# Column sums of squares: adding finished tiles on GpSimd before TensorE sums them

## What is computed

```
x = x + gx1 * _rms_norm(_token_mixer(h, ...), g_post_mix)     # the mixer ends in merged @ w_out
hm = _modulate(x, g_pre_mlp, sx2, cx2)                        # _rms_norm(x) * (1 + scale) + shift
x = x + gx2 * _rms_norm(square(relu(hm @ w1)) @ w2, g_post_mlp)
```

## Time and profile before

| | us |
|---|---|
| timed runs, median of 3 | 4251.79 |
| lowest and highest | 4250.93, 4254.33 |
| the profiled execution | 4245.13 |
| its span, first to last instruction | 4243.4 |
| mean granted TensorE clock in it | 0.917 |

### The profile page before, as it was taken

How to read it: one execution, slowest core, us unless ns; L and a number is a source line. 1 busy time by engine, 2 the same in 40 slices (tenths; PEclk the granted TensorE clock), 3 DMA queues, 4 the chain that set the end, 5 groups by cost and what they waited for, 6 DMA issues and landing times. The chain is left out here.

```text
span 4243.4 us, 47248 instructions
## 1 busy us (share of the span) xinstructions
PE 3803.9 (90%) x18108; PEld 2862.6 (67%) x18108; DVE 1992.6 (47%) x3170; ACT 1441.9 (34%) x2504; POOL 148.6 (4%) x104
## 2 busy tenths in 40 slices
PE   6888898989999999989799998999898877998777
PEld 3888897646777788757556777788786435784435
DVE  1755664655443544316655443544323354333363
ACT  2554333234433222233244433222223433223421
POOL 0000000010000100000100001000100010000010
PEclk9999998999999899899899998999898678997788
DMA  7434452211123222262111122222221000220001
GB/s 292 139 117 152 135 167 101 85 35 45 55 70 100 70 94 95 102 261 99 60 45 45 65 70 85 85 96 98 68 95 60 15 5 30 80 94 25 15 5 60
DMA packets 95535, 362.40 MB, mean 85 GB/s; under 512 B 10976, under 2 KB 11232, under 8 KB 93792
## 3 DMA queue, kind: packets, MB, share of 16 engines
q1 hardware_dynamic: 95328, 359.52, 25.0%
HBM read 352.13 MB, written 7.34 MB: 85 GB/s over the span
## 5 line engine op out<-in xcount | busy, mean ns | idle before, releaser
L365 DVE TENSOR_TENSOR w_lo<-w_raw,w_hi 128x1024 fp32r<-128x1024 f32 x525 | 642.4, 1224 | 932.0 <-ACT w_hi L355 931.6
L379 PE MATMUL banks<-h_hi,w_hi 128*128 128x512 f32 (+1 forms) x2040 | 766.7, 376 | 26.7 <-DVE h_lo L997 9.8
L380 PE MATMUL banks<-h_lo,w_hi 128*128 128x512 f32 (+1 forms) x2040 | 748.0, 367 | 0.0
L381 PE MATMUL banks<-h_hi,w_lo 128*128 128x512 f32 (+1 forms) x2040 | 748.0, 367 | 0.0
L355 ACT ACTIVATE w_hi<-w_raw 128x1024 fp32r<-128x1024 f32 x543 | 570.7, 1054 | 412.1 <-DMA w_raw<-in_stream 404.3
L379 PEld LDWEIGHTS banks<-h_hi,w_hi 128*128 128x128 f32 x2040 | 390.6, 191 | 109.6 <-issue 22.1
L381 PEld LDWEIGHTS banks<-h_hi,w_lo 128*128 128x128 f32 x2040 | 389.3, 191 | 64.8
L380 PEld LDWEIGHTS banks<-h_lo,w_hi 128*128 128x128 f32 x2040 | 390.1, 191 | 60.5 <-issue 0.5
L379 PE MATMUL banks<-merged_hi,w_hi 128*128 128x512 f32 (+1 forms) x960 | 349.9, 364 | 28.5 <-PEq L2312 10.7
L381 PE MATMUL banks<-merged_hi,w_lo 128*128 128x512 f32 (+1 forms) x960 | 346.9, 361 | 0.0
L380 PE MATMUL banks<-merged_lo,w_hi 128*128 128x512 f32 (+1 forms) x960 | 345.7, 360 | 0.0
(11 more groups left out here) (309 smaller groups left out, 5324.9 us busy)
## 6 DMA issues: line engine op xcount, KB each, us to landing
w_raw<-in_stream SPq DMA_DIRECT2D x591, 512.0 KB, 3.5
w_whole<-in_stream SPq DMA_DIRECT2D x48, 512.0 KB, 9.0
x_kept<-x SPq DMA_DIRECT2D x2, 2048.0 KB, 7.5
dft_table<-in_dft SPq DMA_DIRECT2D x2, 2048.0 KB, 8.3
x<-x_kept SPq DMA_DIRECT2D x2, 2048.0 KB, 8.4
x<-in_x SPq DMA_DIRECT2D x1, 2048.0 KB, 12.2
out_x<-x SPq DMA_DIRECT2D x1, 2048.0 KB, 6.2
late_consts<-in_consts SPq DMA_DIRECT2D x1, 1280.0 KB, 5.6
```

The lines of the kernel that those rows point to most:

```text
L365: (by or self.nc.vector).tensor_tensor(self.lo[:, c], self.raw[:, c], self.hi[:, c].bitcast(F32), ALU.subtract)\
L379: self.nc.tensor.matmul(out, w_hi, x_hi, start=start, stop=False)
L380: self.nc.tensor.matmul(out, w_hi, x_lo, start=False, stop=False)
L381: mm = self.nc.tensor.matmul(out, w_lo, x_hi, start=False, stop=stop)
```

## The change

`post_mix` and `post_mlp` get a common tile `squares_total`. GpSimd adds the squares of tiles 0 to 6 into it as they are finished: the first add takes tiles 0 and 1, five more take one tile each (`RowNorm.gather`). TensorE no longer sums each tile. It sums the total behind the last tile of the projection (`sum_gathered`) and then the last tile's squares (`sum_last`), so a norm has two groups of columns in PSUM instead of eight. ScalarE, ahead of square k from the fifth on, waits for GpSimd's add that read the slot. `pre_mlp`, `pre_mix` and `following` stay as they were. On GpSimd's list the gathering for post_mix comes first, the two low parts of chunks move from ahead of the first residual to behind it, and the gathering for post_mlp stands between them and the second residual.

```diff
--- before.py
+++ after.py
@@ -873,18 +873,22 @@
 
 
 
-    def __init__(self, K, name, n_tiles, NT, at, rows_bank):
-        self.K, self.n, self.NT, self.nt = K, n_tiles, NT, NT // P
-        self.sums = K.ps[:, 7, at:at + n_tiles * self.nt]
+    def __init__(self, K, name, n_tiles, NT, at, rows_bank, total=None):
+        self.K, self.n, self.NT, self.nt, self.total = K, n_tiles, NT, NT // P, total
+        self.n_sums = n_tiles if total is None else 2
+        self.sums = K.ps[:, 7, at:at + self.n_sums * self.nt]
         self.rows = K.ps[:, rows_bank, 0:NT]
         self.sq = None
         self.mean, self.rt, self.rstd = (K.take(f"{name}_{t}", [self.nt]) for t in ("mean", "root", "rstd"))
         S = lambda t: K.count_of(f"{name}_{t}")
         self.squared, self.summed, self.averaged = S("squared"), S("summed"), S("averaged")
         self.rooted, self.inverse, self.turned = S("rooted"), S("inverse"), S("turned")
+        self.gathered = S("gathered") if total is not None else None
 
     def square(self, act, k, src):
-        if k >= 4:
+        if k >= 4 and self.total is not None:
+            act.wait_ge(self.gathered.sem, self.gathered.at(max(1, k - 4)))
+        elif k >= 4:
             act.wait_ge(self.summed.sem, self.summed.at(k - 3))
         return self.K.nc.scalar.activation(self.sq[:, k % 4], src, ACT.Square).then_inc(self.squared.sem, 1)
 
@@ -896,8 +900,30 @@
                                          self.K.const("ones")[:, 0:1], start=True, stop=True)
         mm.then_inc(self.summed.sem, 1)
 
+    def gather(self, pool):
+        for k in range(1, self.n - 1):
+            pool.wait_ge(self.squared.sem, self.squared.at(k + 1))
+            if k > 1:
+                pool.wait_ge(self.gathered.sem, self.gathered.at(k - 1))
+            self.K.nc.gpsimd.tensor_tensor(self.total[:], self.sq[:, 0] if k == 1 else self.total[:], self.sq[:, k % 4], ALU.add)\
+                .then_inc(self.gathered.sem, 1)
+
+    def sum_gathered(self, pe):
+        pe.wait_ge(self.gathered.sem, self.gathered.at(self.n - 2))
+        for i in range(self.nt):
+            mm = self.K.nc.tensor.matmul(self.sums[:, i:i + 1], self.total[:, i * P:(i + 1) * P], self.K.const("ones")[:, 0:1],
+                                         start=True, stop=True)
+        mm.then_inc(self.summed.sem, 1)
+
+    def sum_last(self, pe):
+        pe.wait_ge(self.squared.sem, self.squared.at(self.n))
+        for i in range(self.nt):
+            mm = self.K.nc.tensor.matmul(self.sums[:, self.nt + i:self.nt + i + 1], self.sq[:, (self.n - 1) % 4, i * P:(i + 1) * P],
+                                         self.K.const("ones")[:, 0:1], start=True, stop=True)
+        mm.then_inc(self.summed.sem, 1)
+
     def average(self, dve):
-        dve.wait_ge(self.summed.sem, self.summed.at(self.n))
+        dve.wait_ge(self.summed.sem, self.summed.at(self.n_sums))
         self.K.nc.vector.reduce_sum(self.mean[:], self.sums.rearrange("p (k i) -> p i k", i=self.nt), AX_X)\
             .then_inc(self.averaged.sem, 1)
 
@@ -921,9 +947,11 @@
         eng.wait_ge(self.turned.sem, self.turned.at(1))
 
     def close(self):
-        for s, n in ((self.squared, self.n), (self.summed, self.n), (self.averaged, 1), (self.rooted, 1),
+        for s, n in ((self.squared, self.n), (self.summed, self.n_sums), (self.averaged, 1), (self.rooted, 1),
                      (self.inverse, 1), (self.turned, 1)):
             s.advance(n)
+        if self.total is not None:
+            self.gathered.advance(self.n - 2)
         for t in (self.mean, self.rt, self.rstd):
             self.K.give(t)
 
@@ -1024,9 +1052,10 @@
         m = K.sb(scope, "mid", [2, NT])
         sq = K.sb(scope, "squares", [4, NT])
         table = K.sb(scope, "table_load", [1])
-        post_mix = RowNorm(K, "post_mix", KD, NT, 0, 4)
+        total = K.sb(scope, "squares_total", [NT])
+        post_mix = RowNorm(K, "post_mix", KD, NT, 0, 4, total)
         pre_mlp = RowNorm(K, "pre_mlp", KD, NT, 32, 5)
-        post_mlp = RowNorm(K, "post_mlp", KD, NT, 64, 4)
+        post_mlp = RowNorm(K, "post_mlp", KD, NT, 64, 4, total)
         for norm in (post_mix, pre_mlp, post_mlp, following):
             if norm is not None:
                 norm.sq = sq
@@ -1046,9 +1075,8 @@
                 for k in range(KD):
                     W.multiply(pe, K.ps[:, f % 4, 0:NT], (c0 + f) * CHUNK + k, h_hi[:, k, 0:NT], h_lo[:, k, 0:NT],
                                k == 0, k == KD - 1)
-                if f >= 1:
-                    post_mix.sum(pe, f - 1)
-            post_mix.sum(pe, KD - 1)
+            post_mix.sum_gathered(pe)
+            post_mix.sum_last(pe)
             post_mix.turn(pe)
             for f in range(KD):
                 pre_mlp.sum(pe, f)
@@ -1074,9 +1102,8 @@
                             pe.wait_ge(mid_lo_ready.sem, mid_lo_ready.at(8 * turn + k + 1))
                         W.multiply(pe, K.ps[:, 2 + f % 2, 0:NT], (c + 8 + f) * CHUNK + k, mid_hi[:, k], mid_lo[:, k],
                                    k == 0, k == 7)
-                    if turn == turns - 1 and f >= 1:
-                        post_mlp.sum(pe, f - 1)
-            post_mlp.sum(pe, KD - 1)
+            post_mlp.sum_gathered(pe)
+            post_mlp.sum_last(pe)
             post_mlp.turn(pe)
             if following is not None:
                 for f in range(KD):
@@ -1121,10 +1148,12 @@
                     pool.wait_ge(scaled.sem, scaled.at(n + f + 1))
                     nc.gpsimd.tensor_tensor(x[:, f, 0:NT], x[:, f, 0:NT], m[:, f % 2], ALU.add).then_inc(added[1].sem, 1)
 
-            lead.pool(pool, range(up + AHEAD, up + SLOTS))
+            post_mix.gather(pool)
             for sem, value in x_in:
                 pool.wait_ge(sem, value)
             residual(0)
+            lead.pool(pool, range(up + AHEAD, up + SLOTS))
+            post_mlp.gather(pool)
             residual(KD)
 
         @block.vector
```

## The result

The kernel after takes 4219.51 us, the median of four runs (4215.84 to 4220.78). The kernel before, run beside it on the same chip, takes 4251.36 us (four runs, 4247.07 to 4254.33). The ratio is 0.9924, with a 95% interval of 0.9907 to 0.9942, so 31.8 us less. The profiled executions have spans of 4217.1 and 4243.4 us, with the same mean granted clock of 0.917.

What follows compares the result with a forecast made beforehand. TensorE's instruction stream was taken to set each tile's period. Gains of 25.9 us (sums removed) and 7.6 us (splits moved), with adds at 0, made 33.5 us: from 4251.8 to 4218 us, range 4209 to 4230.

Steps and rivals of the forecast that it cites:

- TensorE's stream sets the period of a tile: Out-projections and last MLP turns: sums between products stretch each tile by their own length, 0.85, 0.44 and 0.87 us.
- Part 1: Six norms, post_mix and post_mlp: six tile sums leave TensorE's path in each, together 25.9 us.
- the context MLP taken like its out-projection: Context stage, 256 tokens: same 0.44 us per tile assumed for both projections, 5.3 us together.
- rival 2: Changed projections: period does not shrink because another engine or weight DMA comes up at once; 4244.2 us, chance 0.05.
- the third turn: MLP turn without sums, 5.60 us a tile, read against 6.47 us in the fourth turn with sums.
- Part 2: First residual of each stage: two GpSimd weight splits move behind it, gaining 7.6 us.
- The twin: Second residual of the same stage, no splits in front: 16.64 us to the mean against 18.70, gain 2.06 us, twice.
- the 2.70 us add: VectorE's first add of the first residual, beside GpSimd's splits: 2.70 us instead of 0.69.
- the late odd tiles: First residual: GpSimd's tiles come late because its first add starts only after 4.83 us of splits.
- the 8.8 of the forecast: Context stage, first scaling to the next norm's mean: 8.8 us instead of 12.32, a gain of 3.5 us.
- Part 3: Six norms: 36 new GpSimd adds and the new waits cost 0; bounds nothing to 49.6 us.
- The splits behind the residual: GpSimd's two moved splits delay nobody, costed at 0; at most 2.3 us if short context operations had to wait.

Runs made afterwards that it cites:

- experiment 6: Kernel after, in the last MLP turn ScalarE's square moved behind the next high-part split, cutting a ring of VectorE and ScalarE waits: 4215.34 us, one run.
- experiment 3: Kernel after with GpSimd's two weight splits put back ahead of the first residual: 4226.45 us, ratio 0.9944 to the kernel before.
- Experiment 5: Kernel after with two more GpSimd adds, into a tile nobody reads, ahead of each of the 36: 4220.54 us, ratio 0.9936 to the kernel before.
- experiments 4: Kernel after without GpSimd's adds and the waits for them, TensorE summing tile 6's squares instead of the total: 4217.11 us, ratio 0.9928 to the kernel before.
- experiment 7: Kernel after with the same gathering by GpSimd for norm 'following' in the second block's layer 0: 4212.97 us, ratio 0.9917 to the kernel before.

## Why the prediction was right

It said 4218 us, and 4219.51 was measured. That the two lie 1.5 us apart is partly luck: two executions of the same code differ by 6.6 us, and two misses in the sum are partly offset by a gain in the layers. The steps are what can be judged:

- **TensorE's stream sets the period of a tile.** Right with 512 tokens and in the context's out-projection: the gaps fell to that of the gap without sums, and TensorE's idle list ahead of the total is empty. In the context's last turn TensorE's stream got shorter as well, but VectorE's adds did not keep up with it.
- **Part 1, 25.9 us.** The 512-token terms: 10.2 forecast, 10.5 measured; 10.4 forecast, 10.6 measured. The context's term was 5.3 for both projections; its out-projection gave the full 2.65, its last turn 1.4 to 1.55. The step that failed is "the context MLP taken like its out-projection": 1.1 us went missing there. It is rival 2 in part: other engines come up, the ring of experiment 6, without holding TensorE. The last add starts 1.21 us behind TensorE's last product and not 0.32, which is 0.9 of the 1.1 us. The prediction checked the shorter period only against the out-projection and the third turn, where no square stands in ScalarE's list between the add and the split.
- **Part 2, 7.6 us.** The twin was the right row to read: 2.17 and 2.02 for 2.06 twice. But the 2.70 us add is layer 1's alone, and it adds nothing to the late odd tiles (experiment 3). The context gave 2.9 to 3.0 instead of 3.5. The sum there took the first square to follow the first add. In the kernel after, ScalarE's timeline shows what stood in front of it:

```profile
418.34 1.06 ACT L355 ACTIVATE w_hi<-w_raw 128x1024 fp32r<-128x1024 f32 x1 [1.16 <-DMA w_raw<-in_stream]
419.30 1.22 ACT L893 ACTIVATE squares<-context 128x256 f32<-128x256 f32 x3
```

  The first add ended at 418.63, but ScalarE's second split, whose chunk landed late, ran to 419.40. Experiment 5 shows it from the other side: there the scaling came 1.6 us later, both splits were done by then, and scaling to mean took 8.84 us, the 8.8 of the forecast.
- **Part 3, adds and waits at 0.** Right, by experiments 4 and 5. (In experiment 7's execution TensorE waited 0.41 us for the total in the context's last turn; in those of the kernel after it did not wait.) Adds and splits did collide. Beside an add VectorE's split took 1.49 us instead of 1.23, as the timelines of the kernel after have it, GpSimd's row first:

```profile
2973.43 1.32 POOL L908 TENSOR_TENSOR squares_total<-squares_total,squares 128x512 f32<-128x512 f32 x1 [4.28 <-ACT squares L893]
```

```profile
2974.33 1.49 DVE L365 TENSOR_TENSOR w_lo<-w_raw,w_hi 128x1024 fp32r<-128x1024 f32 x1 [1.65 <-ACT w_hi L355]
```

  The 0.26 us vanish in the slack of two periods.
- **The splits behind the residual** hurt nobody: the time from the mean of `pre_mlp` to the first add of the last turn is 323.9 to 326.5 us with 512 tokens in every kernel, moved or not.
- **The sum.** 33.5 forecast; 10.5 + 10.6 + 4.2 + 7.05 = 32.35 by the rows. The two misses are both in the context stage, and together 1.7 us; the layers of 512 tokens gave 0.5 us more than forecast.

The Trainium skill (SBUF — State Buffer, "SBUF: two separate sides") makes whichever of the two engines starts first hold the shared port for its whole instruction. The starts in the traces agree, and they tell which length the add gets. One split takes 2.35 us. In experiment 3 the first split ends at 2611.78+2.35 = 2614.13; the add has started before that, at 2613.54, and ends 0.55 us behind it, while the second split waits (5.11 us for the pair). In layer 1 of before the first split ends at 2628.43+2.35 = 2630.78, 0.33 us before the add starts, so the add ends 0.55 us behind the second one: 2.70 us. It started later there because the eight products of TensorE ahead of the scaling took 2.08 us at a granted clock of 0.50, where in layer 0 they took 1.17 us at 0.94. The 0.26 us above agree in direction only: the split started 0.42 us before the add ended.

What stays open is why the context's chunk lands late in most of these kernels; no run moved that transfer.

## What to carry to other kernels

Work that TensorE does between the products of a stream that it bounds costs its full length, however small it looks in the shares; find it by comparing the periods of tiles with and without it, and give it to an idle engine when it fits in a period and its result is wanted later than that. Read a diff for what it moves in the engines' lists as well: here a reordering that the change's title doesn't name brought a quarter of the gain. And once TensorE's share of a tile shrinks, look tile by tile for a ring through the other engines, above all in the stage with the shortest period. Before you credit a cut ring with a shorter stage, compare the granted clock of both executions, and look whether the bounding engine had gaps at all: here half or more of a 2.6 us difference was the clock.

## What the runs showed of the hardware

- VectorE's add with both operands in SBUF (0.69 us alone) took 2.70 us behind two GpSimd splits, or 1.14 us where it got in between them, and then the pair took 5.11 us instead of 4.83. It was long where it started after the first split had ended, and short where it started before. Two scalings with an operand in PSUM took 1.41 us in both.
- A tile's column sums (8 records for 512 tokens) cost 0.84 to 0.90 us in the stream at the granted clock of 1.0 (2.4 GHz), and 1.73 us in the bursts at 0.5 (1.2 GHz).
- The same kernel gave profiled spans 6.6 us apart on two executions, nearly all of it outside the stretches that the change shortens; only the rows of a stage could tell a 1 us effect.
